# A high/low split kernel: the high weights' two products in one matmul of 512 columns, and a gate by tanh

## What is computed

```
for l in range(2):                                   # first block
    z = rms_norm(x) @ w_in[l]                        # 16 heads: 6 dilated, 6 neighbourhood, 4 memory
    o = attention of each head (memory heads: keys and values from mem_n @ w_mem_kv[l])
    y = o * silu(gate)                               # the gate is one of the head's four products
    x = x + y @ w_out[l]
z = rms_norm(x) @ w_in_2                             # second block: u, q, k, v, and two gates
y_ssm  = s5_mixer(u);  y_attn = diff_attention(q, k, v)
m = sigmoid(g_s) * (y_ssm @ w_proj_ssm) + sigmoid(g_a) * (y_attn @ w_proj_attn)
x = x + m @ w_out_2
h = rms_norm(x)
x = x + (silu(h @ w_gate) * (h @ w_up)) @ w_down     # 44 blocks of 128 hidden columns
```

## Time and profile before

| what | value |
|---|---|
| median of three runs | 2481.77 us |
| span of the profiled execution, first to last instruction | 2480.0 us |
| TensorE busy | 2440.9 us, 98% |
| VectorE busy | 1689.3 us, 68% |
| ScalarE busy | 1223.0 us, 49% |
| GpSimd busy | 623.0 us, 25% |
| DMA | 485.10 MB, mean 196 GB/s |

### The profile page before, as it was taken

How to read it: one execution, slowest core, us unless ns; L and a number is a source line. 1 busy time by engine, 2 the same in 40 slices (tenths; PEclk the granted TensorE clock), 3 DMA queues, 4 the chain that set the end, 5 groups by cost and what they waited for, 6 DMA issues and landing times.

```text
span 2480.0 us, 50498 instructions
## 1 busy us (share of the span) xinstructions
PE 2440.9 (98%) x18064; PEld 2325.0 (94%) x18064; DVE 1689.3 (68%) x2557; ACT 1223.0 (49%) x1818; POOL 623.0 (25%) x1007
## 2 busy tenths in 40 slices
PE   7999999999999999999999999999999999999999
PEld 7999999999999999999999999999888888888888
DVE  7876676668887777678878875665555555555555
ACT  5444444455566565566665444444444344444443
POOL 3310031257988995210012221111000000000000
PEclk9999999999999999999999999999999999999999
DMA  6765566556556655556466866765766766677764
GB/s 230 232 192 194 183 208 209 183 181 205 188 187 202 199 190 178 178 168 208 162 194 226 271 218 212 221 199 182 199 187 190 187 187 187 186 190 186 186 186 154
DMA packets 225485, 485.10 MB, mean 196 GB/s; under 512 B 22792, under 2 KB 130004, under 8 KB 225120
## 3 DMA queue, kind: packets, MB, share of 16 engines
q1 hardware_dynamic: 182912, 415.29, 54.8%
q10 hardware_dynamic: 31168, 35.66, 4.4%
q0 software_dynamic: 11296, 32.68, 4.3%
HBM read 455.20 MB, written 31.08 MB: 196 GB/s over the span
## 4 chain that ended last, share of the span: by engine, by line
PE 79%; DVE 8%; issue 4%; DMA 4%; ACT 3%; POOL 1%; ACTq 1%; DVEq 0%; POOLq 0%
PE z_ps L2075 15%; PE z_ps L2077 15%; PE z_ps L2076 15%; PE z_ps L2426 6%; PE z_ps L2427 6%; PE z_ps L2432 6%; DVE w_lo L1350 3%; ACT w_hi L729 1%; DMA arena<-na_pad_d 1%; PE o_ps L2114 1%; DMA na_bias_d<-arena 1%; PE o_ps L2461 1%; PE o_ps L2460 1%; PE o_ps L2459 1%; PE v_ps L2461 1%
## 5 line engine op out<-in xcount | busy, mean ns | idle before, releaser
L2075 PE MATMUL z_ps<-x_hi,w_hi 128*128 128x256 f32 x2816 | 814.8, 289 | 17.3 <-DVE w_lo L1343 10.4
L1350 DVE TENSOR_TENSOR w_lo<-w_raw,w_hi 128x1024 fp32r<-128x1024 f32 x520 | 637.4, 1253 | 262.8 <-ACT w_hi L729 261.0
L2077 PE MATMUL z_ps<-x_hi,w_lo 128*128 128x256 f32 x2816 | 798.5, 284 | 0.0
L2076 PE MATMUL z_ps<-x_lo,w_hi 128*128 128x256 f32 x2816 | 798.3, 283 | 0.0
L729 ACT ACTIVATE w_hi<-w_raw 128x1024 fp32r<-128x1024 f32 x520 | 533.9, 1052 | 282.9 <-PE z_ps L2077 241.2
L2075 PEld LDWEIGHTS z_ps<-x_hi,w_hi 128*128 128x128 f32 x2816 | 541.5, 192 | 24.1 <-issue 19.7
L2076 PEld LDWEIGHTS z_ps<-x_lo,w_hi 128*128 128x128 f32 x2816 | 541.7, 192 | 1.2
L2077 PEld LDWEIGHTS z_ps<-x_hi,w_lo 128*128 128x128 f32 x2816 | 541.4, 192 | 0.0
L1965 DVE TENSOR_TENSOR w_lo<-w_raw,w_hi 128x1024 fp32r<-128x1024 f32 x262 | 320.7, 1225 | 314.0 <-ACT w_hi L1190 314.0
L1190 ACT ACTIVATE w_hi<-w_raw 128x1024 fp32r<-128x1024 f32 x262 | 277.7, 1060 | 427.1 <-PE z_ps L2432 269.5
L2426 PE MATMUL z_ps<-w_hi,x_hi 128*128 128x512 f32 x704 | 275.0, 391 | 0.0
(11 more groups left out here) (405 smaller groups left out, 4118.5 us busy)
## 6 DMA issues: line engine op xcount, KB each, us to landing
w_raw<-in_w SPq DMA_DIRECT2D x704, 512.0 KB, 4.3
w_raw<-in_w SPq DMA_DIRECT2D x80, 384.0 KB, 4.9
w_raw<-in_w SPq DMA_DIRECT2D x80, 128.0 KB, 2.9
tab_d<-arena ACTq DMA_DIRECT2D x32, 256.0 KB, 4.0
res<-tab_d POOLq DMA_DIRECT2D x16, 384.0 KB, 5.9
arena<-tab_d POOLq DMA_DIRECT2D x16, 384.0 KB, 6.1
tab_d<-arena ACTq DMA_DIRECT2D x32, 128.0 KB, 2.6
sg_d<-arena ACTq DMA_DIRECT2D x32, 128.0 KB, 5.1
```

Of the source, the lines that this page charges most:

```text
L1350: dve.tensor_tensor(w_lo[:, n % RING, :], w_raw[:, n % RING, :], w_hi[:, n % RING, :].bitcast(F32), ALU.subtract).then_inc(w_lo_ready, 1)
L2075: pe.matmul(z, wh, hi[:, kt, :], start=(first and i == 0), stop=False)
L2076: pe.matmul(z, wh, lo[:, kt, :], start=False, stop=False)
L2077: m = pe.matmul(z, wl, hi[:, kt, :], start=False, stop=(last and i == len(kts) - 1))
```

## The change

1. `x_hi` and `x_lo`, `m_hi` and `m_lo`, `y_hi` and `y_lo` become the two halves of one tensor (`x_both` and so on). Per block of weights, one matmul multiplies `w_hi` with both halves (512 columns, the high result in columns 0 to 255 of the bank, the low one in 256 to 511), and a second one adds `w_lo` x high (256 columns) to the first half. The GLU product keeps its three matmuls; so do the gate and up products of the feed-forward.
2. The two halves of the bank are added on VectorE at every evacuation: by a `tensor_reduce` over a view with the halves innermost and a multiplication after it (`halves_sum`), or by two additions to the residual one after the other. Every such pair has a semaphore `z_added` between.
3. The projections use two banks per block instead of one, and the down product one bank per output block instead of one per chunk. `down` waits before each chunk n for the addition of chunk n - 2; `ffn_down` adds chunk by chunk.
4. The gate of the first block's layers is (tanh(z/2) + 1) z, by a tanh on ScalarE and one operation on VectorE; the factor 0.5 goes into `gated`.
5. The PSUM tensors are declared as two tensors of four banks, and two semaphores at the start are merged.

```diff
-        x_hi = sb("x_hi", [P, KT, T], F32R)
-        x_lo = sb("x_lo", [P, KT, T], F32R)
+        x_both = sb("x_both", [P, 2, KT, T], F32R)
+        x_hi, x_lo = x_both[:, 0], x_both[:, 1]
...
-            def gate_exp(p, g, first=False):
+            def gate_tanh(p, g, first=False):
                 act.wait_ge(z_free, taken(p, 3))
                 if not first:
-                    act.wait_ge(gate_1_ready, g)
-                act.activation(gate_e[:], gate_z[:], ACT.Exp, scale=-1.0).then_inc(gate_e_ready, 1)
+                    act.wait_ge(gate_ready, g)
+                act.activation(gate_e[:], gate_z[:], ACT.Tanh, scale=0.5).then_inc(gate_e_ready, 1)
...
+            def halves_sum(dst, z, p, c):
+
+                job_done(p, c)
+                dve.tensor_reduce(dst, z.rearrange("p a t -> p t a"), AX_X, ALU.add).then_inc(z_added, 1)
+                dve.wait_ge(z_added, added(p, c))
+
             def evac(dst, p, c, scale):
-                job_done(p, c)
-                dve.tensor_tensor(dst, z_ps[c % 4][:, 0, :], scale, ALU.mult).then_inc(z_free, 1)
+                halves_sum(dst, z_ps[c % 4], p, c)
+                dve.tensor_tensor(dst, dst, scale, ALU.mult).then_inc(z_free, 1)
...
             def gate_silu(g):
                 dve.wait_ge(gate_e_ready, g + 1)
-                dve.tensor_scalar(gate_1[:], gate_e[:], 1.0, None, ALU.add).then_inc(gate_1_ready, 1)
-                dve.wait_ge(gate_1_ready, g + 1)
-                dve.reciprocal(gate_r[:], gate_1[:]).then_inc(gate_r_ready, 1)
-                dve.wait_ge(gate_r_ready, g + 1)
-                dve.tensor_tensor(gate[:], gate_z[:], gate_r[:], ALU.mult).then_inc(gate_ready, 1)
+                dve.scalar_tensor_tensor(out=gate[:], in0=gate_e[:], scalar=1.0, in1=gate_z[:], op0=ALU.add,
+                                         op1=ALU.mult).then_inc(gate_ready, 1)
...
             def out_block(p, c, l, n):
                 job_done(p, c)
-                dve.tensor_tensor(res[:, n, :], z_ps[c % 4][:, 0, :], res[:, n, :], ALU.add).then_inc(z_free, 1)
+                dve.tensor_tensor(res[:, n, :], z_ps[c % 4][:, 0, :], res[:, n, :], ALU.add).then_inc(z_added, 1)
+                dve.wait_ge(z_added, added(p, c))
+                dve.tensor_tensor(res[:, n, :], z_ps[c % 4][:, 1, :], res[:, n, :], ALU.add).then_inc(z_free, 1)
...
-                dve.tensor_tensor(pz, z_ps[c % 2][:], sg_in[c % 2], ALU.mult).then_inc(z_free, 1)
+                pair = z_banks[:, 2 * (c % 2):2 * (c % 2) + 2]
+                dve.tensor_reduce(pz, pair.rearrange("p s a t -> p s t a"), AX_X, ALU.add).then_inc(z_added, 1)
+                dve.wait_ge(z_added, added(p - 1, c))
+                dve.tensor_tensor(pz, pz, sg_in[c % 2], ALU.mult).then_inc(z_free, 1)
...
             def ffn_down(base, g, k):
 
-                dve.wait_ge(w_free, RING + base + 2 * k + 2)
-                dve.tensor_tensor(res[:, 4 * k:4 * k + 2, :], d_ps[k % 2][0][:], res[:, 4 * k:4 * k + 2, :], ALU.add)
-                dve.tensor_tensor(res[:, 4 * k + 2:4 * k + 4, :], d_ps[k % 2][1][:], res[:, 4 * k + 2:4 * k + 4, :],
-                                  ALU.add).then_inc(down_used, 1)
+                for s in range(2):
+                    pair, r = a_banks[:, 2 * s:2 * s + 2], slice(4 * k + 2 * s, 4 * k + 2 * s + 2)
+                    dve.wait_ge(w_free, RING + base + 2 * k + s + 1)
+                    dve.tensor_tensor(res[:, r, :], pair[:, :, 0, :], res[:, r, :], ALU.add).then_inc(z_added, 1)
+                    dve.wait_ge(z_added, added(P_FFN - 1, 0) + 8 * g + 2 * k + s)
+                    dve.tensor_tensor(res[:, r, :], pair[:, :, 1, :], res[:, r, :], ALU.add).then_inc(down_used, 1)
...
-                    pe.matmul(z, wh, hi[:, kt, :], start=(first and i == 0), stop=False)
-                    pe.matmul(z, wh, lo[:, kt, :], start=False, stop=False)
-                    m = pe.matmul(z, wl, hi[:, kt, :], start=False, stop=(last and i == len(kts) - 1))
+                    pe.matmul(z, wh, both[:, :, kt, :], start=(first and i == 0), stop=False)
+                    m = pe.matmul(z[:, 0, :], wl, both[:, 0, kt, :], start=False, stop=(last and i == len(kts) - 1))
...
             def down(base, g, k, at):
 
-                if not (isinstance(g, int) and g == 0 and k < 2):
-                    pe.wait_ge(down_used, 4 * g + k - 1)
                 pe.wait_ge(fg_lo, 2 * g + 2)
                 for s in range(2):
                     n = 2 * k + s
+                    if not (isinstance(g, int) and g == 0 and k == 0):
+                        pe.wait_ge(down_used, 8 * g + n - 1)
                     pe.wait_ge(w_lo_ready, base + n + 1)
                     for b in range(2):
-                        z = d_ps[k % 2][s][:, b, :]
+                        z = a_banks[:, 2 * s + b]
                         for kt in range(F_GROUP):
                             c = (F_GROUP * b + kt) * P
                             wh, wl = w_hi[:, n % RING, c:c + P], w_lo[:, n % RING, c:c + P]
-                            pe.matmul(z, wh, y_hi[:, at + kt, :], start=(kt == 0), stop=False)
-                            pe.matmul(z, wh, y_lo[:, at + kt, :], start=False, stop=False)
-                            m = pe.matmul(z, wl, y_hi[:, at + kt, :], start=False, stop=(kt == F_GROUP - 1))
+                            pe.matmul(z, wh, y_both[:, :, at + kt, :], start=(kt == 0), stop=False)
+                            m = pe.matmul(z[:, 0, :], wl, y_hi[:, at + kt, :], start=False, stop=(kt == F_GROUP - 1))
                     m.then_inc(w_free, 1)
```

More of the change, by code:

```diff
@@ L144, in build @@
         scores, probs, probs_t = (part(1, 2, pair) for _ in range(3))
-        gate_z, gate_e, gate_1, gate_r, gate = (part(1, 1, row) for _ in range(5))
+        gate_z, gate_e, gate = (part(1, 1, row) for _ in range(3))
         top[0] = heads_at + 6
@@ L486, in _ @@
             for k in range(4):
-                sp.wait_ge(down_used, 4 * (N_GROUPS - 1) + k + 1)
+                sp.wait_ge(down_used, 8 * (N_GROUPS - 1) + 2 * k + 2)
                 sp.dma_start(out[:, 4 * k:4 * k + 4, :], res[:, 4 * k:4 * k + 4, :]).then_inc(out_stored, 16)
@@ L849, in head_period @@
                 if prev:
-                    gate_exp(p - 1, g - 1, prev and not prev2)
+                    gate_tanh(p - 1, g - 1, prev and not prev2)
                 split_hi(p, 2)
@@ L1392, in gated @@
                 dve.wait_ge(y_hi_ready, g + 1)
-                dve.tensor_tensor(y_f[:], o_ps[:, 0, :], gate[:], ALU.mult).then_inc(y_ready, 1)
+                dve.scalar_tensor_tensor(out=y_f[:], in0=o_ps[:, 0, :], scalar=0.5, in1=gate[:], op0=ALU.mult,
+                                         op1=ALU.mult).then_inc(y_ready, 1)
             def y_lower(g, h):
@@ L2064, in _, with chunk @@
             pe.sem_inc(w_free, RING)
-            def chunk(z, p, n, kts, hi, lo, first, last, wait_kt=None):
+            def chunk(z, p, n, kts, both, first, last, wait_kt=None):
                 pe.wait_ge(w_lo_ready, 8 * p + n + 1)
@@ L2215, in _ @@
                 pe.wait_ge(z_free, 4 * po + 1)
-                z, z1 = z_ps[0][:, 0, :], z_ps[1][:, 0, :]
-                chunk(z, po, 0, range(CH), y_hi, y_lo, True, False, y_there).then_inc(w_free, 1)
-                chunk(z, po, 1, range(CH, HEADS - 1), y_hi, y_lo, False, False, y_there)
+                z, z1 = z_ps[0], z_ps[1]
+                chunk(z, po, 0, range(CH), y_both, True, False, y_there).then_inc(w_free, 1)
+                chunk(z, po, 1, range(CH, HEADS - 1), y_both, False, False, y_there)
                 attn_turn(g)
@@ L2251, in _, with job2 @@
                         out_rest(i)
-            def job2(p, c, hi, lo, wait_kt=None, ring=2):
+            def job2(p, c, both, wait_kt=None, ring=2):
                 pe.wait_ge(z_free, taken(p, c - ring))
-                z = z_ps[c % ring][:, 0, :]
+                z = z_ps[c % ring]
                 for s in range(2):
-                    chunk(z, p, 2 * c + s, range(CH * s, CH * (s + 1)), hi, lo, s == 0, s == 1,
+                    chunk(z, p, 2 * c + s, range(CH * s, CH * (s + 1)), both, s == 0, s == 1,
                           wait_kt).then_inc(w_free, 1)
@@ L2312, in head_2 @@
                     values2(i)
-                job2(p, 1, x_hi, x_lo, ring=4)
+                job2(p, 1, x_both, ring=4)
                 if prev:
@@ L2317, in head_2 @@
                     output_sums(i)
-                job2(p, 2, x_hi, x_lo, ring=4)
-                job2(p, 3, x_hi, x_lo, ring=4)
+                job2(p, 2, x_both, ring=4)
+                job2(p, 3, x_both, ring=4)
                 pe.wait_ge(qk_sq_ready, i + 1)
@@ L2387, in _ @@
                 for s in range(2):
-                    chunk(z_ps[c % 2][:, s, :], P_GLU, 2 * c + s, range(CH), m_hi, m_lo, True, True,
-                          (lambda kt: pe.wait_ge(yg_lo, kt + 1)) if c == 0 and s == 0 else None).then_inc(w_free, 1)
+                    z, n = z_ps[c % 2][:, s, :], 2 * c + s
```

(13 more changed lines are left out.)

105 lines of the change are left out of this document (52 added, 53 removed).

## The result

The changed kernel takes 2685.3 us as a median (2682.7 to 2689.6), 1.0822 times the time before, 95% interval 1.0807 to 1.0836. I had forecast 2604 with a range to 2650: the direction was right, the size too small by 81 us. The profiled execution has a span of 2684.8 us, 204.8 more than before, where my sum gave 122.4.

A forecast was written before the change was run, and what follows sets the result against it. TensorE, busy 98% of the span, was taken as the bound. Span 2480.0 - 40.6 (joined matmuls less VectorE's additions) + 124 (down-product gaps) + 39 (clock) = 2602.4, or 2604 us as a median; range 2548 to 2650.

The forecast's parts named there:

- Part 3: Down product: with one buffer lost, TensorE waits 4.0 us for VectorE's addition, 31 times, +124 us.
- the signs that I had named: Group about 78 us, over 80 with clock; PEclk below 9 in twelve slices; second block's head about 29; 17 table loads.
- Part 4: Down product: the granted clock falls after the new gaps, about 1.6 us lost each time, +39 us, bounds 0 and +50.
- 8 in 10 of 31: Down product: the share of the 31 gaps taken to be followed by a fallen clock, giving +39 us.
- stayed full: Kernel before: the clock kept full speed after 2.45 us of idleness before 1522.77; cited for a 2565 us rival, chance 0.16.
- Part 1: All joined matmuls: each of 4800 saved starts saves 0.0133 us, -64.0 us if TensorE alone decided everywhere.
- Part 2: Evacuations: adding the halves on VectorE costs +0.72 us each; together with the joined matmuls -40.6 us.
- hidden, if those waits absorb it: Layers' heads: VectorE's net +0.9 us per period of 25 to 27.6 us costs nothing; layers keep their 34.1 us saving.
- So VectorE needs 26.1 now: Second block's heads: period 27.63 less 1.5 us of w_hi waits; 29.0 after, +1.4 in 7 periods, +9.8 us.
- 5.8: Projections: us VectorE needs per block after +1.2, against TensorE's 5.55; about today's pace, 3.4 us saving not obtained.
- The tanh's cost of nothing: First block's gates: tanh on ScalarE costs 0, far end 41 us; its longer chain is off TensorE's path.
- the rival of the joined matmul that saves nothing: All joined matmuls: fixed part grows with width, so the 53 us saving still counted falls away; 2655 us, chance 0.06.

The follow-up runs named there:

- Experiments 1: Changed kernel, but in the down product VectorE adds each chunk's sums before splitting the next weights, chunk by chunk: 2503.6 us, ratio 1.0098 to the kernel before.
- experiment 3: Kernel before, nothing joined, but the down product waits before each chunk for the addition two chunks back (two buffers): 2630.4 us, ratio 1.0602.
- Experiment 4: Changed kernel with 28 unused matmuls put into each of the three stops of a group, all groups but the last: 2634.2 us, ratio 1.0623 to before.
- the mended kernel: Changed kernel with VectorE's down-product additions put ahead of the weight splits, chunk by chunk; all joined: 2503.6 us, ratio 1.0098 to the kernel before.
- experiment 7: The mended kernel, but only the first half of each bank evacuated, by one operation, in the second block's heads: 2485.8 us, ratio 1.0019 to before.
- experiment 8: The mended kernel with one of ScalarE's two squares left out in layer 1's output blocks: 2502.9 us, ratio 1.0086 to the kernel before.
- the partial join: Mended order and tanh, matmuls joined only in layer 0, the second block's output product and the down product: 2463.3 us, ratio 0.9929 to before.

## Why the prediction was wrong

- **Part 3, right.** Three stops a group, 31 in all, released by VectorE's addition; 3.81 us idle, or by the starts 4.0 late (1941.29 to 1945.37 in place of 0.12), where I had put 4.0; 117 us idle where I had put 124. Experiments 1 and 3 show the order as the cause, independent of the join. The 0.2 us for waking TensorE stood in no row; here the addition ends at 1945.24 and TensorE starts 0.13 later. Of the signs that I had named, the group's period (84.6) and the 17 table loads came; the second block's head period was 30.2 and not 29, and the clock's digit fell below 9 in only four of the last slices, not in twelve.
- **Part 4, the term was mis-sized.** "8 in 10 of 31" times 1.6 gave 39. Measured: 179.4 - 117.1 = 62.3, or 2.0 for every one of the 31, and beyond the +50 that I had put as the far end. The record of the clock in the trace gives the same: behind the 31 restarts TensorE works 124 us at 1.2 GHz, and full speed would have needed half of that. So both factors were too small. The clock fell after 31 of 31, not 25. And the 1.6 was read from a single restart (half of its 3.4 us is 1.7, besides), while nine stops of 31 leave the clock low for over 4 us of work. Experiment 4 shows 1.9 a stop. The Trainium skill ("TensorE: Matmul & The Clock Gate", section HAM oscillation) describes such a loop, with the loss at each wait; this trace agrees, with 31 of 31. That the clock "stayed full" after 2.45 us of idleness was weak comfort: in the kernel before it fell 1.3 us after the next restart, at 1534.01, with only 2.0 us of idleness before it:

```profile
1535.00:1539.00 4.00, 4.00 (x23) 4.00 (x22) 3.02 (x5) 2.52 (x3) 0.00 (x0) 0.57 0.80 262
```

- **Part 1, the saving per pair was too large.** A joined pair takes 0.3467 or 0.3533 us, constant within a run of pairs; of 4348 pairs in the longer runs of the mended kernel 1671 lie at the lower level and 2647 at the upper. Against 0.360 that is 13 or 7 ns; in the down product with its mean of 0.3532 it is 7, and the feed-forward gives 5.0 instead of 704 x 0.0133 = 9.4. The Trainium skill's 2.5 ns beside the columns for an isolated matmul (same page, section Back-to-back issue gap) is lower still; the measurement decides. The price was read from matmuls of one width in a row; no row had the two widths in turn, as the prediction said of its rival.
- **Part 2, the step that failed most.** I wrote "hidden, if those waits absorb it" for the layers' heads and "So VectorE needs 26.1 now" for the second block's. The waits on w_hi are links of a serial loop (VectorE, ScalarE, VectorE), and don't absorb; this is shown in the second block's heads and layer 1's outputs, and in the layers' heads it is read from TensorE's waits. In the second block's heads the period grew by 2.5 of the added 2.9 us, not by 1.4 (+19.8 for +9.8; experiment 7). In layer 1's outputs I had not looked for a loop at all: without the second addition it takes 6.08 - 0.45 = 5.6 (and 5.60 is what it took before, L1436 at 1011.09 and 1016.69), only 0.1 to 0.2 below TensorE's 16 x 0.360 = 5.76, and +0.45 made it the bound (+6.8 for -3.4; experiment 8). Gates, GLU and projections: +9.1 for -3.4, of which the projections from their fifth block on 5.4. There my "5.8" did not follow from its own rows: TensorE's 5.76 less the waits of 0.51 and 0.41, and 1.2 more, is 6.0, above today's pace; measured were 68.5 / 11 = 6.2 against 63.1 / 11 = 5.7. Price and form of the reduction were right: L1375 takes 0.68 and the next starts 0.72 later; the permuting one takes 0.68 as well.
- **The layers' heads, the largest miss ahead of the feed-forward**: -2.6 for -27.3. By TensorE's waits and the record of the clock in both profiles, 8.8 of the missing 24.7 us are more waiting, 5.3 are work at 1.2 GHz after such waits, which my sum for the layers did not have at all, and the rest, 10.6, is mostly what the pairs saved less. In the first heads of layer 1 TensorE itself waits for the bank that VectorE empties and rotates, which now stands behind the reduction. Its waits from 560 to 700 us were 2.2 us for L1384 (0.2 for GpSimd); now:

```profile
PE z_ps L2151 <- DVE arena L1389: 5.8, 4, 2.0
PE z_ps L2151 <- POOL arena L572: 0.8, 1, 0.8
```

  One of these waits shows a part that the change need not have paid. The bank is read for the last time by the reduction, but `z_free` is counted up only by the last product of the rotation, 1.6 us after the reduction has ended; `evac` gives its bank back after its multiplication too. No run tests an earlier release.

```profile
573.90 0.69 DVE L1375 TENSOR_REDUCE arena<-z_ps 128x256 f32<-128x512 f32 x1
...
575.64 0.52 DVE L1389 TENSOR_TENSOR arena<-arena 64x256 f32<-64x256 f32 x1
...
576.21 0.44 PE L2151 MATMUL z_ps<-ident,arena 128*128 128x128 f32 x2 [1.63 <-DVE arena L1389]
```

- **The tanh's cost of nothing was right, its gain was missed.** No table was added; but I had called the gate's chain "off TensorE's path", and VectorE's chain is in it there, so that the shorter gate gives 10 us alone and made up for 34 us of the join.

Together: feed-forward +20.8 (stops -6.9, clock +23.3, pairs +4.4), layers' heads +24.7, layers' outputs +12.9, second block's heads +10.0, gates to projections +12.5, its output +1.2; 82.1 of 82.4 us. The sum was thus short in every term but one. (In the rival of the joined matmul that saves nothing, "the 53 us" should be 64.0 - 13.6 = 50; its sum does not use them.) Why just these runs of pairs take 0.3533 stays open: it isn't the layout, and the order of the two only moves it. Open too is what the gates and the GLU product lose beside the projections; no run takes them apart.

## What to carry to other kernels

When a change takes a buffer away, read the consumer's program in order: the release must not stand behind work that needs the next buffer's own progress. Moving two additions ahead of two splits was worth 180 us of 2685. An engine that is idle part of the time can still pace its stage: go once round the loop of waits, and compare its length with the bound's period, before calling idle time a cover. Small waits of the bounding engine cost more than their length where the clock falls after them: count both. And add work only in stages where that loop has room; the partial join is the fastest version here, the full one is slower than none.

## What the runs showed of the hardware

- A pair of matmuls of 512 and 256 columns with two weights repeats at 0.3467 or 0.3533 us and keeps its level to the end of the run. Two neighbouring runs in the mended kernel: 14 pairs from 95.64 to 100.59, 0.3536 each, and 30 pairs from 102.37 to 112.78, 0.3470.

```profile
95.64 0.40 PE L2091 MATMUL z_ps<-x_both,w_hi 128*128 128x512 f32 x1
...
100.59 0.40 PE L2091 MATMUL z_ps<-x_both,w_hi 128*128 128x512 f32 x1
...
102.37 0.40 PE L2091 MATMUL z_ps<-x_both,w_hi 128*128 128x512 f32 x1
...
112.78 0.39 PE L2091 MATMUL z_ps<-x_both,w_hi 128*128 128x512 f32 x1
```

- After 31 stops of 3.0 to 3.8 us the granted clock was low each time, for 3.4 us in 22 cases and for 6.8 in nine; in the nine it fell 0.6 to 1.7 us before work began again. The loss was 2.0 us a stop, and 1.8 with stops of 3.1 us (experiment 3). After 2.0 us of idleness in the kernel before it fell as well (1534.01).
- Matmuls whose sums nobody reads paid for themselves: 756 of them made the kernel 51 us faster.
